# Stick-breaking running sums in two fp32r parts instead of fp32

## The reference

```python
z = jnp.einsum('bqhd,bkhd->bhqk', qb, k) * scale
visible = k_pos[None, :] < q_pos[:, None]
log_stay = jnp.where(visible, jax.nn.log_sigmoid(-z), 0.0)
log_pass = lax.cumsum(log_stay, axis=3, reverse=True) - log_stay
w = jnp.where(visible, jnp.exp(jax.nn.log_sigmoid(z) + log_pass), 0.0)
o = jnp.einsum('bhqk,bkhd->bqhd', w, v)
```

## Time and profile before

| what | value |
|---|---|
| median of 3 runs | 1054.65 us (1054.28 to 1054.81) |
| the profiled execution | 1054.8 us, its span 1053.0 us |
| TensorE busy | 1042.0 us, 99% of the span |
| VectorE busy | 629.2 us, 60% |
| ScalarE busy | 507.7 us, 48% |
| mean granted clock of TensorE | 0.999 |
| HBM traffic | 169.43 MB read |

### The profile page before, as it was taken

How to read it: one execution, slowest core, us unless ns; L and a number is a source line. 1 busy time by engine, 2 the same in 40 slices (tenths; PEclk the granted TensorE clock), 3 DMA queues, 4 the chain that set the end, 5 groups by cost and what they waited for, 6 DMA issues and landing times.

```text
span 1053.0 us, 19997 instructions
## 1 busy us (share of the span) xinstructions
PE 1042.0 (99%) x8108; PEld 1007.5 (96%) x8108; DVE 629.2 (60%) x859; ACT 507.7 (48%) x707; POOL 11.0 (1%) x21
## 2 busy tenths in 40 slices
PE   9999999999999999999999999999999999999997
PEld 8999999999999999999999999999998899999886
DVE  5765553476565776555437765553489777765533
ACT  5643443446464555435335644443447755544433
POOL 0000000000000000000000000000011000000000
PEclk9999999999999999999999999999999999999999
DMA  7665545513332446455451564555513244655551
GB/s 322 206 233 166 191 163 174 186 40 121 121 120 86 155 165 234 161 170 189 161 181 63 206 229 159 179 181 165 188 49 121 85 157 166 238 195 180 179 180 40
DMA packets 24533, 171.26 MB, mean 163 GB/s; under 512 B 2976, under 2 KB 2976, under 8 KB 4384
## 3 DMA queue, kind: packets, MB, share of 16 engines
q1 hardware_dynamic: 24048, 169.49, 46.5%
q10 hardware_dynamic: 432, 1.00, 0.2%
HBM read 169.43 MB, written 1.05 MB: 162 GB/s over the span
## 4 chain that ended last, share of the span: by engine, by line
PE 96%; DVE 1%; ACT 1%; DMA 0%; issue 0%; DVEq 0%; POOL 0%; SPq 0%; ACTq 0%; POOLq 0%
PE ps L1068 25%; PE ps L1069 25%; PE ps L1070 25%; PE ps L1104 3%; PE ps L1113 3%; PE ps L1106 3%; PE ps L1404 2%; PE ps L1405 2%; PE ps L1403 2%; PE ps L1206 1%; PE ps L1225 1%; PE ps L1471 1%; PE ps L1337 1%; PE ps L1310 1%; PE ps L1173 1%; PE ps L1325 1%
## 5 line engine op out<-in xcount | busy, mean ns | idle before, releaser
L474 ACT CAST w_hi<-raw 128x1024 fp32r<-128x1024 f32 x312 | 312.9, 1048 | 397.0 <-PE ps L1070 302.3
L701 DVE TENSOR_TENSOR w_lo<-raw,w_hi 128x1024 fp32r<-128x1024 f32 x312 | 370.3, 1225 | 191.8 <-ACT w_hi L474 191.5
L1068 PE MATMUL ps<-y_hi,w_lo 128*128 128x272 f32 (+1 forms) x1458 | 422.0, 289 | 0.8 <-DVE pre_ms L730 0.6
L1070 PE MATMUL ps<-y_lo,w_hi 128*128 128x272 f32 (+1 forms) x1458 | 419.2, 288 | 0.0
L1069 PE MATMUL ps<-y_hi,w_hi 128*128 128x272 f32 (+1 forms) x1458 | 417.6, 286 | 0.0
L1068 PEld LDWEIGHTS ps<-y_hi,w_lo 128*128 128x128 f32 x1458 | 274.8, 188 | 2.7 <-DVE w_lo L701 1.0
L1069 PEld LDWEIGHTS ps<-y_hi,w_hi 128*128 128x128 f32 x1458 | 274.8, 189 | 0.2
L1070 PEld LDWEIGHTS ps<-y_lo,w_hi 128*128 128x128 f32 x1458 | 274.9, 189 | 0.0
L1069 PE MATMUL ps<-h_hi,w_hi 128*128 (+1 forms) x528 | 152.5, 289 | 0.0
L1070 PE MATMUL ps<-h_lo,w_hi 128*128 (+1 forms) x528 | 152.0, 288 | 0.0
L1068 PE MATMUL ps<-h_hi,w_lo 128*128 (+1 forms) x528 | 151.5, 287 | 0.0
(11 more groups left out here) (142 smaller groups left out, 996.0 us busy)
## 6 DMA issues: line engine op xcount, KB each, us to landing
raw<-in_panels_dram SPq DMA_DIRECT2D x156, 1024.0 KB, 4.9
first<-in_first_dram SPq DMA_DIRECT2D x3, 784.0 KB, 6.9
xT<-in_x_dram SPq DMA_DIRECT2D x1, 1088.0 KB, 13.5
out_dram<-fT SPq DMA_DIRECT2D x4, 256.0 KB, 2.0
const<-in_const_dram ACTq DMA_DIRECT2D x1, 920.0 KB, 10.0
first<-in_first_dram SPq DMA_DIRECT2D x2, 392.0 KB, 3.7
gain_row<-in_row_dram SPq DMA_DIRECT2D x1, 512.0 KB, 5.6
gains<-in_gains_dram ACTq DMA_DIRECT2D x1, 48.0 KB, 3.6
```

What stands on the lines that cost most here:

```text
L474: nc.scalar.copy(w_hi[:, g % SLOTS, part], raw_part(g, part)).then_inc(hi_ready, 1)
L701: nc.vector.tensor_tensor(w_lo[:, g % SLOTS, part], raw_part(g, part), w_hi[:, g % SLOTS, part].bitcast(F32), ALU.subtract).then_inc(lo_re ...
L1068: nc.tensor.matmul(dst, w_lo[:, slot, pc], yh, start=first, stop=False, skip_group_check=shared)
L1070: return nc.tensor.matmul(dst, w_hi[:, slot, pc], yl, start=False, stop=last, skip_group_check=shared)
```

## The change

`softplus` writes an unpadded `sp`. ScalarE rounds it to fp32r (`sp_high`, into `sp_hi`, which lies on the same memory as `e`) and VectorE forms the remainder in place (`sp_low`, `sp_lo`, on the memory of `sp`). `running_sums` multiplies both parts by fp32r copies of `tri` and `ones`, which ScalarE makes once (`sums_w`). Each matmul covers both heads of the pair: for each part 256 columns twice, 288 columns twice, and 64 columns twice, where before there were, for each head, fp32 matmuls of 272, 144, 144 and 32 columns and one of 32 for both. The sums lie differently in two PSUM banks, so that `log_weights` is three subtractions in place of two. `z` takes the padding that `sp` had. `soft` of pair p waits for the sums of pair p-2 (`c_done`) instead of its softplus. The tables of halves are as they were.

```diff
@@ ScalarE
+                    def sp_high(p):
+                        a.wait_ge(sp_ready, p + 1)
+                        nc.scalar.copy(sp_hi[:, p % 2], sp[:, p % 2]).then_inc(sph_ready, 1)
...
                         if p >= 2:
-                            a.wait_ge(sp_ready, p - 1)
+                            a.wait_ge(c_done, p - 1)
...
+                    for n, name in enumerate(("tri", "ones")):
+                        nc.scalar.copy(sums_w[:, n, :], cst(name)).then_inc(sums_w_ready, 1)
...
                         hi_halves(2 + sum(SB_HI[:st]), SB_HI[st])
                         if 1 in at:
                             save_v(at[1])
+                        for k in (1, 2):
+                            if k in at:
+                                sp_high(2 * at[k] + k - 1)
                         for k in (0, 1):
                             if k in at:
                                 soft(2 * at[k] + k)
@@ VectorE
+                    def sp_low(p):
+                        v.wait_ge(sph_ready, p + 1)
+                        nc.vector.tensor_tensor(sp_lo[:, p % 2], sp[:, p % 2], sp_hi[:, p % 2].bitcast(F32),
+                                                ALU.subtract).then_inc(spl_ready, 1)
...
-                        nc.vector.tensor_tensor(w[:, r, :, SB_PAD + 16:], z[:, r, :, 16:],
-                                                ps[:, C_BANK:C_BANK + 2, 16:SB_W], ALU.subtract)
...
+                        nc.vector.tensor_tensor(main_cols(w[:, r]), main_cols(z[:, r]), sums_p, ALU.subtract)
+                        c0, c1 = SB_PAD + 144, SB_PAD + 288
+                        nc.vector.tensor_tensor(w[:, r, :, c0:c1], z[:, r, :, c0:c1], sums_q[:, :, 0:144], ALU.subtract)
+                        nc.vector.tensor_tensor(end_cols(w[:, r]), end_cols(z[:, r]),
+                                                sums_q[:, :, 144:176].rearrange("p a (s n) -> p a s n", s=2),
                                                 ALU.subtract).then_inc(d_ready, 1)
...
                         for k in (0, 1):
                             if k in at:
                                 logits(2 * at[k] + k)
+                        for k in (1, 2):
+                            if k in at:
+                                sp_low(2 * at[k] + k - 1)
                         if 1 in at:
                             save_v(at[1])
@@ TensorE, running_sums
-                        pe.wait_ge(sp_ready, p + 1)
+                        pe.wait_ge(spl_ready, p + 1)
...
+                        for i, part in enumerate((high, low)):
+                            src = part.rearrange("p a (s n) -> p a s n", n=16)
+                            nc.tensor.matmul(sums_p[:, :, 0, :], tri, part[:, :, 16:144], start=(i == 0), stop=(i == 1),
+                                             skip_group_check=True)
+                            nc.tensor.matmul(sums_p[:, :, 1, :], tri, part[:, :, 288:416], start=False, stop=(i == 1),
+                                             skip_group_check=True)
+                            nc.tensor.matmul(n0b, tri, part[:, :, 144:288], start=(i == 0), stop=False,
+                                             skip_group_check=True)
+                            nc.tensor.matmul(n0b, ones, part[:, :, 288:432], start=False, stop=False,
+                                             skip_group_check=True)
+                            nc.tensor.matmul(ends, tri, src[:, :, 0::26, :], start=False, stop=False,
+                                             skip_group_check=True)
+                            mm = nc.tensor.matmul(later, ones, part[:, :, 0:16].unsqueeze(2).broadcast_to([P, 2, 2, 16]),
+                                                  start=False, stop=(i == 1), skip_group_check=True)
```

More of the change, by code:

```diff
@@ L201, in build @@
         fT = sb("fT", [P, KT, L])
+        with ExitStack() as under:
+            sp_hi = under.enter_context(nc.sbuf_tensor("sp_hi", [P, 2, 2, SB_W], F32R))
         sq = sb("sq", [P, KT, L])
@@ L235, in build @@
             v_tok = mix_sb("v_tok", [P, 3, D])
-            z = mix_sb("z", [P, 2, 2, SB_W])
-            sp = mix_sb("sp", [P, 2, 2, SB_PAD + SB_W])
+            z = mix_sb("z", [P, 2, 2, SB_PAD + SB_W])
+            with ExitStack() as under:
+                sp_lo = under.enter_context(nc.sbuf_tensor("sp_lo", [P, 2, 2, SB_W], F32R))
+            sp = mix_sb("sp", [P, 2, 2, SB_W])
+            sums_w = mix_sb("sums_w", [P, 2, P], F32R)
             o_hi = mix_sb("o_hi", [P, KT, L], F32R)
@@ L262, in build, with main_cols, end_cols @@
         w = fT[:].rearrange("p a b -> p (a b)").rearrange("p (r a n) -> p r a n", r=2, a=2)
+        sums_p = ps[:, 4, :].rearrange("p (s a n) -> p a s n", s=2, a=2)
+        sums_q = ps[:, 5, 0:352].rearrange("p (a n) -> p a n", a=2)
+        def main_cols(ap):
+            return ap.rearrange("p a (s n) -> p a s n", n=272)[:, :, :, 128:256]
+        def end_cols(ap):
+            return ap.rearrange("p a (s n) -> p a s n", n=16)[:, :, 7::26, :]
         def raw_part(g, part):
@@ L344, in build @@
         sp_ready = sem("sp_ready")
+        sph_ready = sem("sph_ready")
+        spl_ready = sem("spl_ready")
+        sums_w_ready = sem("sums_w_ready")
         c_done = sem("c_done")
@@ L439, in _ @@
             for r in range(2):
-                nc.gpsimd.memset(sp[:, r, :, 0:SB_PAD], 0.0).then_inc(pad_zero, 1)
                 nc.gpsimd.memset(w[:, r, :, 0:SB_PAD], 0.0).then_inc(pad_zero, 1)
@@ L810, in logits @@
                             v.wait_ge(d_ready, p - 1)
-                        nc.vector.scalar_tensor_tensor(out=z[:, p % 2], in0=ps[:, Z_BANK:Z_BANK + 2, 0:SB_W],
+                        nc.vector.scalar_tensor_tensor(out=z[:, p % 2, :, SB_PAD:], in0=ps[:, Z_BANK:Z_BANK + 2, 0:SB_W],
                                                        scalar=SCALE, in1=mask, op0=ALU.mult,
@@ L818, in softplus @@
                             v.wait_ge(c_done, p - 1)
-                        nc.vector.scalar_tensor_tensor(out=sp[:, p % 2, :, SB_PAD:], in0=z[:, p % 2], scalar=0.0,
+                        nc.vector.scalar_tensor_tensor(out=sp[:, p % 2], in0=z[:, p % 2, :, SB_PAD:], scalar=0.0,
                                                        in1=e[:, p % 2], op0=ALU.max,
                                                        op1=ALU.add).then_inc(sp_ready, 1)
+                    def sp_low(p):
+                        v.wait_ge(sph_ready, p + 1)
+                        nc.vector.tensor_tensor(sp_lo[:, p % 2], sp[:, p % 2], sp_hi[:, p % 2].bitcast(F32),
+                                                ALU.subtract).then_inc(spl_ready, 1)
                     def log_weights(p):
@@ L849, in lo_halves @@
                             lo_half(t.g0 + 4 + i // 2, i % 2)
-                    v.wait_ge(pad_zero, 4)
+                    v.wait_ge(pad_zero, 2)
                     for st in range(SB_TILES + SB_FILL):
@@ L1195, in running_sums @@
                             pe.wait_ge(vb_saved_d, p // 2 + 1)
[L1196 to L1213, removed]
@@ new lines, in running_sums @@
+                        tri, ones = sums_w[:, 0, :], sums_w[:, 1, :]
+                        high, low = sp_hi[:, p % 2], sp_lo[:, p % 2]
+                        if p == 0:
+                            pe.wait_ge(sums_w_ready, 2)
+                        n0b = sums_q[:, :, 0:144]
+                        ends = sums_q[:, :, 144:176].rearrange("p a (s n) -> p a s n", s=2)
+                        later = sums_q.rearrange("p a (s n) -> p a s n", n=16)[:, :, 8::2, :]
+                        for i, part in enumerate((high, low)):
[12 more added lines that the diff above has]
+                                                  start=False, stop=(i == 1), skip_group_check=True)
```

6 lines of the change are left out of this document (2 added, 4 removed).

## The result

The changed kernel takes 1067.63 us (median of 4 runs, 1064.78 to 1069.43) against 1054.72 us for the kernel before (4 runs, 1054.28 to 1054.81): 1.0119 times as long, 95% interval 1.0107 to 1.0131. Slower was right; the size was not: 12.9 us instead of 6.8, and the median lies above the range. The profiled execution is the quickest of the four, 1064.78 us with a span of 1062.7.

What follows compares the result with a forecast made beforehand. TensorE was taken as the bound, nearly without a gap. 1054.8 us profiled + 4.65 (about 14 of new idle against 9.6 saved) + 2.1 for the clock = 1061.5 us; range 1056 to 1066.

Steps and rivals of the forecast that it cites:

- TensorE's saving: In running_sums, fp32r matmuls replacing fp32 were to save 1.2 us a call, 9.6 us over 8 calls.
- switch back: After each running_sums call, 0.08 us for returning from fp32 to the panel matmuls was counted as saved.
- its load time for the small matmuls: In running_sums, the skill's weight-load time put each 64-column matmul at 0.107 us rather than 0.09, saving 9.1 us.
- The stalls: TensorE waits before even pairs' values behind the new queue order: about 14 us new idle, +4.65 us net of the saving.
- The clock: TensorE's clock was to fall once, in group 1's idle stretch of 6.5 us, costing 2.1 us.
- the 4.3 us: Time from the end of TensorE's work to the clock's fall at the kernel's end, compared with group 1's idle stretch.
- The sliding-window part: The second layer's sliding-window mixer, whose code the change leaves alone; the prediction had no term for it.
- Rival B: In the stick-breaking part the stalls come and the clock stays: 1059.3 us; chance 0.30.
- C: The new chain before values has cover and TensorE's saving stands: 1045 us; chance 0.07, its milder form 0.06.
- D: In running_sums, fp32r with strided operands runs at fp32's 1.84 ns a column: 4.5 us a call, 1074 us; chance 0.04.
- The panel load of stage 5: In group 1, this load was to be issued at 267.8 instead of 266.15 us, after the sums of pair 2 start.

Runs made afterwards that it cites:

- the best kernel: The change with ScalarE's and VectorE's queue orders repaired in stages k=2, ScalarE's also in k=3, and 96 do-nothing waits on TensorE's queue: 1047.3 us, ratio 0.9931.
- the padded change: The change with 96 more instructions on TensorE's queue, waits for a semaphore that has long been passed: 1065.2 us, ratio 1.0098.
- the filler kernel: The change with matmuls that nobody reads put into TensorE's idle time before values of pairs 0, 2, 4 and 6: 1059.27 us, ratio 1.0043.
- the 96 waits: Do-nothing semaphore waits added to TensorE's queue in the stick-breaking projections; added to the change alone: 1065.2 us, ratio 1.0098.
- without the split: The change with sp_high and sp_low left out, softplus writing fp32r itself and the sums adding that one part twice: 1051.75 us, ratio 0.9978.

## Why the prediction was wrong

- **TensorE's saving**: 9.6 us forecast. TensorE's busy time in the part, at full clock throughout, fell from 144.77 to 136.41 in the best kernel, 8.4 us (8.7 by the starts of the eight calls). So the step was 0.9 to 1.2 us too high: 0.64 of it is the "switch back", which is not saved, and the rest are calls of 1.45 us on the mean instead of 1.36, less what every second fp32 call took above the 2.48 us (2.59).
- The Trainium skill (TensorE: Matmul & The Clock Gate, "LDWEIGHTS (loading the stationary operand)") gave 9.1 us by its load time for the small matmuls. That is nearer, but not for its reason: 64 columns cost 0.03 us beside a like matmul and 0.11 before a longer one, 0.07 on the mean and not 0.107.
- **The stalls**: right in place, cause and size. Idle before the even pairs' values: 2.5, 6.5, 2.5, 2.8 forecast, 2.12, 6.46, 2.18, 2.33 measured. The stalls come out 1.2 us smaller in sum, the saving about as much: that the two together are so near, +4.65 forecast and +3.98 measured, is in part luck.
- **The clock, the step that failed**: The forecast allowed one fall. "An idle stretch of 6.5 us is longer than the 4.3 us; so I expect one fall in group 1", 2.1 us. The profiled execution lost 2.87 us there and 1.71 in group 2, behind an idle stretch of 2.18 us that was taken to be safe; the padded change lost 8.6 us in four. The 4.3 us were read at the end of the kernel, the only fall in the trace, and made a threshold of one event; stretches of 2 us are followed by a fall in some executions and not in others. A term for all four groups, of 0 to 8.6 us by these runs, would have just held the median (1054.65 + 4.65 + 8.6 = 1067.9).
- **The sliding-window part, put at nothing in the prediction**: +1.84 us in the profiled execution and +3.05 in the second run of the same kernel.
- The account of the profiled execution: 3.98 + 4.58 + 1.84 = 10.4 us, less 0.3 in the last part (197.83 instead of 198.15) and 0.4 at the start (207.59 instead of 208.00) = 9.7, the difference of the spans. That execution, 1064.78 us, would have lain inside the range. The median of the four runs is 2.9 us above it; their mean clocks of 0.990 to 0.992 against its 0.993 point to more time at half rate, which no profile of them shows.
- Rival B, a clock that stays, is refuted by the half-rate stretches and by the filler kernel, whose part is 3.7 us shorter with them gone; C is what the best kernel makes true, at 1047.3 instead of 1045; D is out by the timeline. The panel load of stage 5 was late as forecast.

## What to carry to other kernels

When an operation is added to a queue written by hand, ask of each instruction behind it what it now waits for: here two cheap operations of 1 us tied the critical subtraction to a panel load, and putting the critical one first turned +12.9 into -7.2 us (with the 96 waits). On a kernel bound by TensorE, price every new idle stretch of the length seen here (about 2 us and up) with a possible fall of the clock on top (half of the work done at half rate), and treat a spread between runs as its sign. Before a difference of 2 us is explained by an edit, look whether it lies in a part that the edit touches.

## What the runs showed of the hardware

- Half-rate stretches of 3.41, 6.83 and 10.24 us, behind or from within idle stretches of 1.9 to 6.5 us; some idle stretches of 2.0 to 2.3 us were followed by none. Their sum was 13.65 us in both profiles of the change, in different places, and 20.47 us with 96 instructions more that do nothing. The 24 filler matmuls in the idle time removed all of them.
- With 95 or 96 instructions fewer on one queue an untouched part took 1.2 to 3.1 us longer (94.2 to 95.9 us in seven kernels, 92.8 to 93.0 in six); in the changed kernel its last wait is for a panel load of 7.0 us instead of 4.9.
- The first matmul behind the short ones is followed by the next only after 0.20 to 0.21 us instead of 0.12 (266.85 to 267.05, 267.57 to 267.78; the earlier trace rows behind the fp32 sums). It is no matter of another operand: without the split, where both passes read the same tile, it is 0.20 us as well (265.19 to 265.39). What causes it stays open.
